# Attention stages reordered, expert routing moved into their ends, weights fetched a stage ahead, and the first expert-row gathers rescheduled, in a five-stage fp32 kernel

## What is computed

```python
x = layer_norm(ALPHA * x + att, ln1_g[layer], ln1_b[layer])
h = x.reshape(B * S, D)
expert, gate = route(h, w_router, b_router)      # softmax(h @ w_router), best group, two best in it
ffn = moe_ffn(h, expert, gate, w_gate[layer], w_up[layer], w_down[layer]).reshape(B, S, D)
x = layer_norm(ALPHA * x + ffn, ln2_g[layer], ln2_b[layer])
```

## Time and profile before

| | |
|---|---|
| time, median of 3 runs | 2290.49 us (2288.29 to 2294.23) |
| the profiled execution: its time | 2287.45 us |
| its span, all engines | 2285.6 us |
| TensorE busy | 1826.9 us (80%) |
| VectorE, ScalarE, GpSimd busy | 805.7, 421.9, 289.7 us |
| moved from memory | 762.40 MB |
| expert weights | 192 loads of 2048 KB |
| gathers | 256, 270.16 MB |

### The profile page before, as it was taken

How to read it: one execution, slowest core, us unless ns; L and a number is a source line. 1 busy time by engine, 2 the same in 40 slices (tenths; PEclk the granted TensorE clock), 3 DMA queues, 4 the chain that set the end, 5 groups by cost and what they waited for, 6 DMA issues and landing times. The chain is left out here.

```text
span 2285.6 us, 22782 instructions
## 1 busy us (share of the span) xinstructions
PE 1826.9 (80%) x9140; PEld 909.8 (40%) x9140; DVE 805.7 (35%) x1881; ACT 421.9 (18%) x980; POOL 289.7 (13%) x280
## 2 busy tenths in 40 slices
PE   9999997865556545569779988888699599888885
PEld 7577884521111111126444333333377333333332
DVE  3735156677777777622320100000213301000002
ACT  2371123221212112112111000000124100000001
POOL 1000022444444444400000000000000000000000
PEclk9999998977776787779779999999799799999998
DMA  7125458999999999955359999999552699999995
GB/s 241 74 111 198 171 194 359 415 421 421 421 421 421 421 421 418 421 223 208 129 225 426 426 427 427 427 426 426 221 232 103 248 427 427 427 426 428 427 427 230
DMA packets 83703, 762.40 MB, mean 334 GB/s; under 512 B 10926, under 2 KB 14737, under 8 KB 22530
## 3 DMA queue, kind: packets, MB, share of 16 engines
q1 hardware_dynamic: 46146, 490.66, 51.6%
q0 software_dynamic: 37440, 270.16, 28.7%
HBM read 759.74 MB, written 1.05 MB: 333 GB/s over the span
## 5 line engine op out<-in xcount | busy, mean ns | idle before, releaser
L2182 PE MATMUL bank<-arena 128*64 128x512 f32 x3072 | 680.6, 595 | 88.7 <-DMA arena<-in_w_up 58.7
L801 PE MATMUL bank<-arena 64*64 64x512 f32 x2048 | 345.0, 832 | 253.1 <-ACT arena L569 253.1
L2182 PEld LDWEIGHTS bank<-arena 128*64 128x64 f32 x3072 | 212.3, 137 | 544.3 <-issue 385.5
L1090 DVE CUSTOM_DVE_ANT_0 arena<-arena 128x1024 f32<-128x1024 f32 x256 | 313.5, 1225 | 173.7 <-DMA arena<-in_peer_uv,arena 171.9
L379 POOL DMA_INDIRECT arena<-in_peer_uv,arena x256 | 280.1, 1094 | 671.0 <-PE bank L801 300.6
L801 PEld LDWEIGHTS bank<-arena 64*64 64x64 f32 x2048 | 99.2, 187 | 490.5 <-ACT arena L569 294.6
L2325 DVE TENSOR_TENSOR arena<-arena,bank 128x512 f32<-128x512 f32 x32 | 22.0, 688 | 700.8 <-PE bank L2182 700.8
L607 PE MATMUL bank<-arena 128*128 128x272 f32 (+2 forms) x768 | 145.4, 349 | 0.5 <-ACT arena L411 0.3
L607 PEld LDWEIGHTS bank<-arena 128*128 128x128 f32 x768 | 126.2, 191 | 20.4 <-issue 3.2
L569 ACT ACTIVATE arena<-arena 128x64 f32<-128x64 f32 x256 | 68.1, 336 | 150.8 <-DVE arena L1102 150.8
L2087 POOL IOTA arena<- 128x128 f32 x2 | 0.5, 242 | 750.6 <-issue 750.6
(11 more groups left out here) (378 smaller groups left out, 1494.7 us busy)
## 6 DMA issues: line engine op xcount, KB each, us to landing
arena<-in_w_gate SPq DMA_DIRECT2D x64, 2048.0 KB, 35.5
arena<-in_w_up SPq DMA_DIRECT2D x64, 2048.0 KB, 29.9
arena<-in_w_down SPq DMA_DIRECT2D x64, 2048.0 KB, 35.0
arena<-in_w_in SPq DMA_DIRECT2D x14, 2048.0 KB, 9.1
arena<-in_w_out SPq DMA_DIRECT2D x2, 4096.0 KB, 23.1
arena<-in_wq SPq DMA_DIRECT2D x4, 2048.0 KB, 13.9
...
arena<-in_peer_uv,arena POOLq DMA_INDIRECT x256, 15.9
```

The costliest lines, as they stand in the source:

```text
L801: m = pe.matmul(bank[banks[t][half]][to:to + HALF, :], DIAG[lo:lo + HALF, k + j, :], row[lo:lo + HALF, D + half * 512:D + (half + 1) * 512 ...
L1090: v.tensor_tensor_reduce(SCR, SLOT[slot_of[j]][:, 0:D], XF[u // PH], 1.0, 0.0, ALU.mult, ALU.add, DOTS[:, u, k:k + 1]).then_inc(s_dot, 1)
L2182: x = pe.matmul(bank[b][j * C:(j + 1) * C, :], operand[:, c, j * C:(j + 1) * C], RING[s % AHEAD][:, c % (DC // 2), j, :], start=(c == 0), ...
```

## The change

In the peer the first 48 picks use eight slots, the later queries are split into halves of a head pair, and routing, merging and the rest of the mixer are moved between the first quads. `attention_stage` becomes `gating_stage` for layer 0: queries and memory first, attention of four heads written between the gate projections, the output product in two parts. The three weights of the dilated stage are loaded by the expert stage ahead of it, into ring slots that it has left. Routing moves into a class `Router` whose parts run at the end of both attention stages: TensorE turns the raw residual, the gain is multiplied into the router's weights beforehand, and `vector_logits` applies mean and root afterwards; `keep_busy` adds matmuls on the identity. The scaled copy `Y`, the further gate columns and the number of passes are made after the first selection matrices (`after_first`).

```diff
+def keep_busy(pe, bank, ident, n):
+    for _ in range(n):
+        pe.matmul(bank[:, 0:P], ident, ident, start=True, stop=True)
...
-    SLOTS_FIRST, SLOTS_ALL, PICKS_FIRST = 8, 12, 24
+    SLOTS_FIRST, SLOTS_ALL, PICKS_FIRST = 8, 12, 48
...
-    QUERIES = ((0, 0, 0, 2, 4, 5), (0, 0, 2, 4, 6, 7), (0, 1, 0, 4, 4, 5), (1, 0, 0, 4, 4, 5), (1, 1, 0, 4, 4, 5),
-               (0, 2, 0, 4, 4, 5), (0, 3, 0, 4, 4, 5), (1, 2, 0, 4, 4, 5), (1, 3, 0, 4, 4, 5))
+    QUERIES = ((0, 0, 0, 2, 4, 5), (0, 0, 2, 4, 6, 7)) + tuple(
+        (t, k, lo, lo + 2, 4, 5) for t, k in ((0, 1), (0, 2), (1, 0), (1, 1), (0, 3), (1, 2), (1, 3)) for lo in (0, 2))
     NQ = len(QUERIES)
-    QUERIES_AFTER = {3: 3, 4: 4, 5: 5, 7: 6, 9: 7, 11: 8}
+    QUERIES_AFTER = {0: 3, **{g + 1: g for g in range(4, NQ)}}
+    LAST_WITH = [1 + max(g for g in range(NQ) if QUERIES[g][1] == k) for k in range(4)]
     SCORES_AFTER = {n + 1: g for n, g in QUERIES_AFTER.items()}
...
-                        if n < 2:
-                            w_out(1, n)
-                        if n == 3:
+                        if n in (1, 2):
+                            w_out(1, n - 1)
+                        if n == 5:
...
             ve.wait_ge(s_ev, PROJ_TILES + LATE_TILES)
-            merge(1)
+            route(1, 0)
+            route(1, 1)
+            merge(1, 0)
...
+                        if j == 2:
+                            route(1, 2)
+                            merge(1, 1)
+                        v.tensor_tensor_reduce(XF[1] if n == 0 else SCR, SLOT[slot_of[j]][:, 0:D], XF[u // PH], 1.0, 0.0, ALU.mult, ALU.add,
...
-                    if u == 0:
-                        route(1 + q // 2, q % 2 * 2)
-                        route(1 + q // 2, q % 2 * 2 + 1)
-                    elif u + 2 < UNITS:
-                        route(u + 2, q)
...
+                    if n == 1:
+                        route(1, 3)
+                    elif n in (2, 3):
+                        route(2, 2 * (n - 2))
+                        route(2, 2 * (n - 2) + 1)
+                    elif u and u + 2 < UNITS:
+                        route(u + 2, q)
+                    if n == 4:
                         residual(1)
...
+    def tensor(self, te, pe, s_res):
+        K = self.K
+        for t in range(TT):
+            te.wait_ge(s_res, 2 * t + 2)
+            for n in range(2):
+                for c in range(4):
+                    m = pe.transpose(K.bank[self.turn_banks[2 * t + n]][:, c * P:(c + 1) * P],
+                                     K.h_res[:, t, (4 * n + c) * P:(4 * n + c + 1) * P], K.ident)
+                m.then_inc(self.s_mm, 1)
+        te.wait_ge(self.s_vec, SUMS_READ)
+        for t in range(TT):
+            for c in range(DC):
+                if c % 4 == 0:
+                    te.wait_ge(self.s_xt, 2 * t + c // 4 + 1)
+                m = pe.matmul(K.bank[self.logit_bank][:, t * NE:(t + 1) * NE], self.XT[:, c, t * P:(t + 1) * P], self.GWR[:, c, :],
+                              start=(c == 0), stop=(c == DC - 1))
+            m.then_inc(self.s_mm, 1)
+        keep_busy(pe, K.bank[self.idle_bank], K.ident, 28)
+        te.wait_ge(self.s_vec, CHOSEN)
...
+        keep_busy(pe, K.bank[self.idle_bank], K.ident, 12)
...
+    def vector_logits(self, ve, do, v, mean, rstd):
+        K = self.K
+        ve.wait_ge(self.s_mm, LOGITS_MM + TT)
+        ve.wait_ge(self.s_vec, SUMS_READ)
+        for t in range(TT):
+            do(v.scalar_tensor_tensor(self.LGT[:, t, :], self.GWB[:, 0:NE], mean[:, t:t + 1],
+                                      K.bank[self.logit_bank][:, t * NE:(t + 1) * NE], ALU.mult, ALU.add))
+        for t in range(TT):
+            do(v.scalar_tensor_tensor(self.LGT[:, t, :], self.LGT[:, t, :], rstd[:, t:t + 1], self.GWB[:, NE:], ALU.mult, ALU.add))
+        v.tensor_reduce(K.NM_, self.LGT, X_AXIS, ALU.max, negate=True).then_inc(self.s_vec, 1)
...
+            sp.dma_start(WMV, rows("w_mem_v0")).then_inc(s_mem, 16)
+            router.sync(sp)
+            for kind in "abc":
+                w_in(kind, *CHUNKS[kind])
...
+            for n in range(6):
+                project(*JOBS[n])
+                if n == 3:
+                    router.tensor_weights(te, pe, bank[7])
+            te.wait_ge(s_pj, job("mk", 1) + 1)
+            for p in range(MPAIRS):
+                scores(p)
+            project("a", 0)
+            turn(0)
+            turn(1)
+            project("b", 0)
+            te.wait_ge(s_pj, job("mv", 1) + 1)
+            te.wait_ge(s_sc, MEM_H)
+            values(0)
+            values(1)
+            project("a", 1)
+            project("b", 1)
+            project("c", 0)
+            te.wait_ge(s_gv, 1)
...
+            for i, n in enumerate((2, 0, 1)):
+                for g in range(4 * n, 4 * n + 4):
+                    m = pe.matmul(bank[GATED[i]][:, g % 4 * P:(g % 4 + 1) * P].rearrange("p (a b) -> p a b", a=TT), SGW[:, g, :],
+                                  UG[:, :, SG_W + g * HD:SG_W + (g + 1) * HD], start=True, stop=True)
+                m.then_inc(s_gm, 1)
+            mix_turn(0)
+            project("c", 1)
+            mix_turn(1)
+            te.wait_ge(s_wo, 16)
+            te.wait_ge(s_mixt, 2)
+            for n in range(2):
+                out_part(0, n, 0)
             te.wait_ge(s_pj, len(JOBS))
...
+            out_part(1, 0, 0)
+            mix_turn(2)
+            out_part(1, 1, 0)
+            mix_turn(3)
+            te.wait_ge(s_mixt, 4)
+            for t in range(TT):
+                for n in range(2):
+                    out_part(t, n, 1)
+            router.tensor(te, pe, s_res)
...
+            ve.wait_ge(s_root, 1)
+            do(v.reciprocal(RSTD, RSTD))
+            router.vector_logits(ve, do, v, MEAN, RSTD)
+            do(v.scalar_tensor_tensor(H[:, 0, :], CENT[:, 0, :], RSTD[:, 0:1], LB, ALU.mult, ALU.add))
+            router.vector_choose(ve, do, v)
+            do(v.scalar_tensor_tensor(H[:, 1, :], CENT[:, 1, :], RSTD[:, 1:2], LB, ALU.mult, ALU.add))
+            router.vector_gates(do, v)
+            router.vector_ranks(ve, do, v)
...
-            for n in range(2):
-                sp.dma_start(WV[:, :, n * VW:(n + 1) * VW], rows("w_v")[:, :, n * VW:(n + 1) * VW]).then_inc(s_vw[n], 16)
-            sp.dma_start(WK, rows("w_k")).then_inc(s_kw, 16)
-            sp.dma_start(WIN, d["w_in1"].rearrange("(c p) n -> p c n", p=P)).then_inc(s_qw, 16)
...
+                steps = sp.value_load(NSTEPS[0:1, 0:1], min_val=FIRST_FREE, max_val=FIRST_FREE + (PASSES - 1) * (PAIRS * HALVES))
+                names = ("w_v", "w_k", "w_in1")
+                for n, (to, name) in enumerate(zip(dilated_weights(K), names)):
+                    sp.wait_ge(s_step, steps + 2 * n if n else steps)
+                    src = d[name].rearrange("(c p) n -> p c n", p=P) if n == 2 else d[name][0].rearrange("p (c n) -> p c n", c=DC)
+                    sp.dma_start(to, src).then_inc(K.s_att_w[n], 16)
...
+                if isinstance(m, int):
+                    after_first()
...
+            def after_first():
+                for t in range(TT):
+                    v.tensor_scalar(Y[:, t, :], H[:, t, :], ALPHA, None, ALU.mult).then_inc(s_acc, 1)
```

922 lines of the change are left out of this document (460 added, 462 removed).

## The result

The changed kernel takes **2230.43 us** (median of 4 runs, 2227.05 to 2232.43) against 2289.65 for the kernel before, measured beside it (median of 4): a ratio of 0.9736, 95% interval 0.9717 to 0.9756, so 59 us (2.6%) faster. Forecast were 2227 us, between 2212 and 2246. The profiled execution took 2231.76 us (span 2230.0), 55.7 less than that of before.

What follows compares the result with a forecast made beforehand. Weight streams bound the expert stages, a TensorE and VectorE chain the stretches between; 8 + 19.5 + 16.6 + 4 + 15.2 = 63.3 us off 2287.45 gives 2224.2, plus 3.0 for the median: 2227 us, range 2212 to 2246.

Steps and rivals of the forecast that it cites:

- Peer, 8 us: Gather stream: earlier row sums save 3 us, the hole at 395 to 400 goes for 4.8; between 3 and 10.
- no routing before the weights: Peer, VectorE's first quad: routing moved from ahead of the weights, part of starting the row sums 3 us sooner.
- The late hole: Peer, 395 to 400: a gather waited 9.0 us for query matmuls; 48 picks on eight slots would save 4.8 us.
- Attention stage 0, 19.5 us: Chain put between projections saves 20.4, clock 3.0, first load 2.7, less waits 4.6 and hops 2.0; between 14 and 24.
- Last matmul to first step: Behind both attention stages: first step at 23.3 us, but the load queue sets the end, saving 16.6 and 15.2 us.
- Dilated stage, 4 us: First projection no longer waits for `w_v`, 3.1 us, and about 1 less of low clock; between 3 and 5.5.
- (a): Peer: eight slots for 48 picks open equally long new holes at quads 2 to 11, no gain; 2241 us, chance 0.10.
- (b): Attention stage 0: ScalarE late at two places makes projections wait, half of the 20.4 us lost; 2237 us, chance 0.08.
- (c): Tails behind attention: TensorE's clock falls to 0.5 despite added matmuls, 8 us over both; 2235 us, chance 0.07.
- (d): No gain at all: streams slow, each expert stage ending 30 us late through prefetched weights sharing the queue; chance 0.02.
- (e): Expert stage: differently rounded logits give an expert 65 tokens, repeating the pass for 471 us; 2698 us, chance 0.02.
- (f): Attention stage 0: ScalarE table switches cost the page's 2.66 us each, not 1.28; 2230 us, chance 0.02.

Runs made afterwards that it cites:

- rounds_late: Changed kernel with attention stage 0's memory-head scores, exps, transposes and values behind all projections instead of between them; 2242.2 us, ratio 0.9799.
- early_8: Changed kernel with expert loads 6 and 7 asked for by the attention stages, right behind the output product's last matmul; 2221.0 us, ratio 0.9690.
- hold_72: Changed kernel with 72 more identity matmuls on TensorE between the barrier and the first packing of each expert stage; 2250.7 us, ratio 0.9816.
- hold_24: Changed kernel with 24 more identity matmuls on TensorE between the barrier and the first packing of each expert stage; 2234.9 us, ratio 0.9751.
- no_keep_busy: Changed kernel without the 28 and 12 identity matmuls that TensorE does beside the choice and the ranks; 2229.7 us, ratio 0.9737.

## Why the prediction was right, and where it was off

- **Total.** Right in sign, 3.4 us too low, inside its range. The steps are those of the forecast; the miss is one cost not foreseen and small errors that partly cancel, so the closeness of the total is partly luck. The one profiled pair misses by more, 55.7 us saved for 63.3, because the execution of before was 2.2 us shorter than its median and that of the changed kernel 1.3 longer. Taken over all executions the pieces are 7.2 + 20.0 + 15.5 - 2.5 + 4.5 + 14.7 = 59.4 us (the 20.0 and 4.5 from means of the table's columns), and the medians differ by 59.2.
- **Peer, 8 us.** Right: 7.2 by nine executions against two. That share should be near 1 from gather 8 on was too much to ask: holes of 5.8 us in sum stay between 310 and 480 in the mean of nine (old front stage: 13.1, mean of two). Gather 8 comes 1.7 us sooner behind the first (24.45 in the mean against 26.2 and 26.1), not 3, partly because the step "no routing before the weights" uncovered a table load of 1.28 us that routing had hidden (VectorE waits 1.48 us for ScalarE before the weights, 0.28 before the change). The late hole gave what was counted on, though its wait did not go: it moved to gather 50, where the DMA engines mostly stay busy through it.
- **Attention stage 0, 19.5 us.** 20.7 measured (19 to 21 over the executions), 112.8 us against "some 114". The waits came as named, on TensorE's timeline of the changed kernel:

```profile
1003.41 7.14 PE L1545 MATMUL bank<-arena 128*128 128x256 f32 x32 [1.70 <-DMA arena<-in_w_in]
1012.43 7.14 PE L1545 MATMUL bank<-arena 128*128 128x256 f32 x32 [1.87 <-DMA arena<-in_w_mem_v]
...
1081.39 10.54 PE L1587 MATMUL bank<-arena 128*128 128x512 f32 x24 [2.34 <-ACT arena L1495]
...
1096.92 14.00 PE L1587 MATMUL bank<-arena 128*128 128x512 f32 x32 [0.69 <-ACT arena L1495]
```

2.34 for the mix behind ScalarE's gelu (forecast 2.5), 0.69 before the second part (0.8), 1.87 for the memory's weights (0.9), none for the gate's root (0.4), and 1.70 for `w_in` at the start, where 3.85 - 2.7 = 1.15 had been left. The estimate of 2.0 for hops was not needed. `rounds_late` shows the cause for 12 us of it, order and clock together; the rest is not separated.
- **Last matmul to first step.** 23.8 us against 23.3, and the queue's bound behind it: 469.2 and 468.6 against 468.1. `early_8` and `hold_72` show that the queue sets the end, with a cover of 4.1 to 4.3 us. I wrote some 3, though my own terms give 4.4: load 8 asked for at 26.8 and 436.9 behind it make 463.7, against 468.1.
- **End of the first expert stage, 0 forecast, 2.5 lost.** The step that failed: I let the early weights cost nothing here, since they fill DMA engines that had been idle (share 0.01 in the earlier trace rows). VectorE's gap at the branch grew from 3.23 to 5.81 us with them. That the loads do it is shown by three placements of them; that it is through VectorE's instructions is the likely reading, not shown.
- **Dilated stage, 4 us.** 5.5 in this execution, 3 to 5.7 over them: the wait for `w_v` is gone (0.69 in place of 4.05), which gives 3.4, and the rest is clock. It is also what makes the scatter: the first ten us of the projections, in the changed kernel and in `hold_24`:

```profile
1609.50:1619.50 10.00, 10.00 (x31) 5.98 (x32) 1.32 (x4) 0.49 (x1) 0.00 (x0) 1.00 0.66 228
1607.40:1617.40 10.00, 10.00 (x25) 5.77 (x26) 1.32 (x4) 0.49 (x1) 0.00 (x0) 0.81 0.66 228
```

In six kernels of the table the clock is up from the start, the 48 matmuls of 384 columns take 27.81 us and the stage 129.2 to 129.5; in the seven others, with granted clocks of 0.75 to 0.82 here, they take 29.5 to 30.3 us. What decides between the two no run shows.
- **Rivals.** (a) fell: no holes at quads 2 to 11 that add up to the old. (b) fell: TensorE waits 3.0 us for ScalarE in the stage, less than the 5 that would have spoken for it. (c) fell as worded, the clock stays up; `no_keep_busy` shows that it would have cost nothing here. (d) did not come: the stage's end lost 2.5 us, not 30. Nor did (e): each expert stage has its 96 steps, one pass. (f) fell, on ScalarE's timeline:

```profile
1064.50 1.28 ACT L1489 ACT_TABLE_LOAD   x1
1065.80 0.20 ACT L1489 ACTIVATE arena<-arena 128x2 f32<-128x2 f32 x1
1066.02 1.28 ACT L1459 ACT_TABLE_LOAD   x1
```

The root follows its table load at once. The Trainium skill (ScalarE: Activation LUTs, What ACT_TABLE_LOAD costs) gives 2.66 us for a switch with its drain; no drain shows here, before or behind the load, and a switch costs 1.28.
